# A streaming encoder layer: the channel mean of a LayerNorm summed by accumulating matmuls instead of vector adds

## What is computed

```
h = rmsnorm(x);  q, k, v, u_a, u_b, gates = split(h @ w_in)
u = u_a * sigmoid(u_b)
y = causal_depthwise_conv(u, width 31) + b_dw        # 1024 channels
mu = mean(y, over the 1024 channels)                 # one mean per token
yc = y - mu
y  = yc * rsqrt(mean(yc*yc) + 1e-6) * ln_g + ln_b
conv = silu(y) @ w_conv_out
m = sigmoid(gA) * attention(q, k, v) + sigmoid(gB) * conv
x = x + rmsnorm(m @ w_out);  x = x + rmsnorm(swiglu(rmsnorm(x)))
```

## Time and profile before

| | |
|---|---|
| time, median of 3 runs (range) | 3239.17 us (3236.28 to 3239.52) |
| the profiled execution: time, span | 3239.52 us, 3237.4 us |
| mean granted TensorE clock | 0.991 |
| TensorE matmul busy | 3144.0 us, 97% |
| VectorE busy | 1555.5 us, 48% |
| ScalarE, GpSimd busy | 1065.4 us (33%), 511.7 us (16%) |
| the chain that ended last | TensorE 79%, VectorE 3%, ScalarE 2% |

### The profile page before, as it was taken

How to read it: one execution, slowest core, us unless ns; L and a number is a source line. 1 busy time by engine, 2 the same in 40 slices (tenths; PEclk the granted TensorE clock), 3 DMA queues, 4 the chain that set the end, 5 groups by cost and what they waited for, 6 DMA issues and landing times.

```text
span 3237.4 us, 42868 instructions
## 1 busy us (share of the span) xinstructions
PE 3144.0 (97%) x16983; PEld 2683.5 (83%) x16983; DVE 1555.5 (48%) x2757; ACT 1065.4 (33%) x1905; POOL 511.7 (16%) x543
## 2 busy tenths in 40 slices
PE   8989989999999999999999999999999999999998
PEld 6768878878887878888887888888899898899987
DVE  7987754445796631003497652002289655200013
ACT  5666432234346421003255532002235542200012
POOL 4930000000471000000083000000057100100000
PEclk9999999999999999999999999999999999999999
DMA  8864568777653355555554344555554332445443
GB/s 279 279 222 170 220 238 293 284 279 283 227 188 137 118 194 183 190 188 208 216 187 169 118 169 175 189 195 208 184 197 176 135 114 109 166 172 182 170 156 125
DMA packets 176486, 622.66 MB, mean 192 GB/s; under 512 B 20656, under 2 KB 26672, under 8 KB 175776
## 3 DMA queue, kind: packets, MB, share of 16 engines
q1 hardware_dynamic: 175328, 619.53, 53.3%
q10 hardware_dynamic: 960, 0.40, 0.0%
HBM read 480.41 MB, written 139.54 MB: 191 GB/s over the span
## 4 chain that ended last, share of the span: by engine, by line
PE 79%; DVE 3%; ACT 2%; DMA 1%; POOL 1%; issue 1%; SPq 0%; DVEq 0%; POOLq 0%; ACTq 0%
PE PS L791 51%; PE PS L843 7%; PE PS L845 7%; PE PS L844 7%; PE PS L825 2%; PE PS L932 2%; PE PS L920 1%; DVE PS L1466 1%; PE PS L951 1%; POOL sq_sum L733 1%; PE PS L952 1%; PE PS L953 1%; PE PS L772 1%; DMA out_y_prompt<-x 1%; ACT act_hi L1238 0%
## 5 line engine op out<-in xcount | busy, mean ns | idle before, releaser
L791 PE MATMUL PS<-h_hi,w_hi 128*128 128x512 f32 (+1 forms) x3328 | 1064.3, 353 | 17.0 <-DVE u L1711 3.9
L791 PE MATMUL PS<-h_hi,w_lo 128*128 128x512 f32 (+1 forms) x3328 | 1065.1, 353 | 0.0
L791 PE MATMUL PS<-h_lo,w_hi 128*128 128x512 f32 (+1 forms) x3328 | 1054.8, 350 | 0.0
L791 PEld LDWEIGHTS PS<-h_hi,w_hi 128*128 128x128 f32 x3328 | 586.0, 189 | 101.9 <-issue 21.2
L791 PEld LDWEIGHTS PS<-h_lo,w_hi 128*128 128x128 f32 x3328 | 585.1, 189 | 90.7 <-issue 1.7
L791 PEld LDWEIGHTS PS<-h_hi,w_lo 128*128 128x128 f32 x3328 | 586.4, 189 | 82.0
L727 POOL TENSOR_TENSOR y<-y,prod 128x512 f32<-128x512 f32 (+1 forms) x333 | 408.4, 1253 | 188.8 <-ACT prod L1216 176.5
L1466 DVE SCALAR_TENSOR_TENSOR PS<-u,dw,PS 128x512 f32<-128x512 f32 (+1 forms) x604 | 434.6, 775 | 7.0
L1868 DVE TENSOR_TENSOR f<-PS,tmp 128x512 f32<-128x512 f32 (+1 forms) x88 | 61.5, 698 | 662.0 <-PE PS L791 643.3
L843 PE MATMUL PS<-w_hi,f_hi 128*128 128x512 f32 x748 | 297.7, 398 | 5.8 <-DVE f L1868 5.4
L845 PE MATMUL PS<-w_hi,f_lo 128*128 128x512 f32 x748 | 295.3, 395 | 0.0
(11 more groups left out here) (195 smaller groups left out, 3631.2 us busy)
## 6 DMA issues: line engine op xcount, KB each, us to landing
w_lo<-lo_dram SPq DMA_DIRECT2D x372, 512.0 KB, 4.3
w_hi<-hi_dram SPq DMA_DIRECT2D x372, 512.0 KB, 3.3
w_raw<-in_w_stream SPq DMA_DIRECT2D x124, 512.0 KB, 4.6
hi_dram<-w_hi SPq DMA_DIRECT2D x124, 512.0 KB, 4.4
lo_dram<-w_lo SPq DMA_DIRECT2D x124, 512.0 KB, 3.9
x<-in_x_prompt SPq DMA_DIRECT2D x4, 2048.0 KB, 12.4
xs<-in_x_prompt SPq DMA_DIRECT2D x12, 512.0 KB, 5.1
out_y_prompt<-x SPq DMA_DIRECT2D x3, 2048.0 KB, 10.6
```

Of the source, the lines that this page charges most:

```text
L791: last = nc.tensor.matmul(PS[:, k0 + off, 0:n], w, x[:, k, c0:c0 + n], start=first and k == 0, stop=stop and k == KT - 1)
```

## The change

The sum over the channel tiles is no longer made by VectorE. TensorE multiplies `ones` with each of the 8 tiles of y itself and lets the products accumulate in the same PSUM bank. In blocks 0 to 2 five of the eight matmuls (tiles 0, 2, 4, 1, 3) are issued at ln 1, two steps earlier than before, and three (tiles 6, 7, 5) at ln 3. In block 3 all eight are issued at ln 3. Before each tile TensorE waits for the tap that ends it, in place of the one wait for `y_summed`. The wait for the residual of the block before (`pn_ok`) moves with the first of them.

```
-            def channel_means(b, ypieces):
-
-                pe.wait_ge(y_summed, b + 1)
-                for c0, n, off in ypieces:
-                    last = nc.tensor.matmul(PS[:, mean_bank(b) + off, 0:n], ones[:], sq_sum[:, c0:c0 + n],
-                                            start=True, stop=True)
-                last.then_inc(mu_done, 1)
+            def channel_means(b, ypieces, cts, first, last_one):
+
+                for ct in cts:
+                    if vector_taps(b, ct) < TAPS:
+                        pe.wait_ge(prod_used, adds_done(b, ct))
+                    else:
+                        pe.wait_ge(conv_step, taps_done(b, ct))
+                    for c0, n, off in ypieces:
+                        last = nc.tensor.matmul(PS[:, mean_bank(b) + off, 0:n], ones[:], y[:, ct, c0:c0 + n],
+                                                start=first and ct == cts[0], stop=last_one and ct == cts[-1])
+                if last_one:
+                    last.then_inc(mu_done, 1)
...
-                        if ln == 3:
+                        if ln == 1 and not ext(b):
                             if b:
                                 pe.wait_ge(pn_ok, post_tile(b - 1, tiles(b - 1) - 1, 1) + 1)
-                            channel_means(b, ypieces)
+                            channel_means(b, ypieces, (0, 2, 4, 1, 3), True, False)
+                        if ln == 3 and not ext(b):
+                            channel_means(b, ypieces, (6, 7, 5), False, True)
+                        if ln == 3 and ext(b):
+                            channel_means(b, ypieces, (0, 2, 4, 1, 3, 6, 7, 5), True, True)
...
-            def sum_tiles(b):
-
-                yw = YW if ext(b) else T
-                dve.wait_ge(conv_step, taps_before(b + 1))
-                total, rest = sq_sum[:, 0:yw], (4, 6, 7, 1, 3, 5)
-                link(TT(total, y[:, 0, 0:yw], y[:, 2, 0:yw], ALU.add))
-                for ct in rest:
-                    if vector_taps(b, ct) < TAPS:
-                        dve.wait_ge(prod_used, adds_done(b, ct))
-                    ins = TT(total, total, y[:, ct, 0:yw], ALU.add)
-                    if ct != rest[-1]:
-                        link(ins)
-                ins.then_inc(y_summed, 1)
...
-                    if ln == 3:
-                        sum_tiles(b)
```

More of the change, by code:

```diff
@@ L218, in build @@
         sbias_in = sem("sbias_in")
-        y_summed = sem("y_summed")
         yn_ok, ahi_ok, afull_ok, alo_ok = sem("yn_ok"), sem("ahi_ok"), sem("afull_ok"), sem("alo_ok")
```

## The result

| | before | after |
|---|---|---|
| median of the timed runs, us | 3238.86 (3236.28 to 3239.52, 4 runs) | 3257.41 (3253.90 to 3260.78, 4 runs) |
| profiled execution: time, span | 3239.52, 3237.4 | 3250.26, 3248.2 |

The ratio is 1.0059, 95% interval 1.0046 to 1.0072: 19 us slower, with 15 to 23 in the interval. Forecast were 3254 us and a range of 3246 to 3262. The profiled execution of the changed kernel is the fastest of all its executions, only 10.7 us above its counterpart; the first experiment shows much of what made it so.

The account below looks back on a forecast made before the run. The prediction took TensorE, busy 97% of the span, to bound the kernel. Its terms, -2.1 us in block 0, +11.0 in blocks 1 and 2, +5.8 in block 3, gave +14.7: 3254 us, range 3246 to 3262.

Parts of the forecast that it names:

- What bounds the kernel: Whole kernel: TensorE's matmuls cover 97% of the span, so work added there costs its full price.
- The price of a mean, 0.88 us and 1.09: TensorE's issue time per mean: 0.88 us in block 1, 1.09 us in block 3 with its two matmuls.
- Blocks 1 and 2, +5.5 each: Per block, seven more means cost 6.16 us and a shorter wait for the squares returns 0.65 us.
- Block 3, +5.8: In block 3, seven more means cost 7.6 us and a shorter wait for the squares returns 1.8 us.
- Block 0, -2.1: In block 0, losing the stall for VectorE's sum and the reduced clock behind it gains 2.1 us.
- The stretch of 14.68 us: Block 0 before: end of step 28 to end of next step, 14.68 us, against 12.57 us after.
- it moves with that step and stays: Block 0's wait before the squares follows ScalarE's last three squares, so it was to remain unchanged.
- The moved waits at ln 1: TensorE's waits for tiles 0, 2, 4, 1, 3 cost nothing, with a margin of 4.9 us in block 1.
- The cheap mean: Rival: successive means overlap down to 0.46 us each, giving 3242.4 us, no visible difference; chance 0.08.
- the late tile: Rival: GpSimd finishes tile 3 late, TensorE stands some 4 us per block at ln 1, 3270 us or above; chance 0.06.
- The faster rival: Rival: VectorE's freed time shortens the start of attention, -11.2 us, to 3228 us; chance 0.05.
- the rivals that give "the same": Outcomes within 0.2%: cheap means, chance 0.08, and a partial gain at attention's start, 0.04; stated together as 0.10.

Follow-up runs that it names:

- the first experiment: The changed kernel run again with no edit, against the kernel before: 3257.39 us, ratio 1.0054.
- the added half alone: The kernel before with its one mean matmul issued eight times at ln 3, VectorE's sum kept: 3262.5 us, ratio 1.0071.
- the removed half alone: The kernel before without VectorE's sum, its one mean matmul taking tile 7 alone: 3235.5 us, ratio 0.9991.

## Why the prediction was right, point by point

- *What bounds the kernel.* Right. With the added half alone +23 us, with the removed half alone -3 us, and by its trace none of that in blocks 1 to 3 up to the squares, where the sum was hidden under TensorE.
- *The price of a mean, 0.88 us and 1.09.* Right: 0.858 and 1.08 in sequence. The Trainium skill's isolated gap of 0.216 us for a matmul of 512 columns ("TensorE: Matmul & The Clock Gate", "Back-to-back issue gap") would be 0.43 for the two records of a mean, and the run with doubled means shows twice that. For the ordinary matmuls, 0.230 us apart, the same rule is nearly right.
- *Blocks 1 and 2, +5.5 each.* Right: +5.4 in the trace, 10.4 us timed for the two. The waits for squares fell to 0.63 us (0.75 forecast).
- *Block 3, +5.8.* Right up to the squares, +5.8. A little came back behind them that was not in the sum. After a stall of 2.6 us the two profiles of the kernel before ran at the lower clock, after one of 0.67 us the changed kernel did not. First the second profile of the kernel before, then the changed one, windows that begin behind the squares:

```profile
2526.00:2528.00 2.00, 2.00 (x7) 1.30 (x8) 0.41 (x1) 0.00 (x0) 0.00 (x0) 0.66 0.71 281
2528.00:2530.00 2.00, 2.00 (x10) 2.00 (x10) 1.18 (x3) 1.57 (x3) 0.00 (x0) 0.50 0.00 0
```

```profile
2546.00:2548.00 2.00, 2.00 (x11) 1.52 (x12) 0.75 (x2) 1.27 (x1) 0.00 (x0) 1.00 0.81 277
2548.00:2550.00 2.00, 2.00 (x18) 2.00 (x17) 1.18 (x2) 1.91 (x3) 0.00 (x0) 1.00 0.62 248
```

  Ten and eighteen matmuls in the same two microseconds; about 1.5 us in all. It is not certain to happen: of six profiles with a single mean in block 3, three had the lower clock behind that stall (of 2.60, 2.61 and 2.55 us) and three kept the higher (2.52, 2.54 and 2.62 us). The length of the stall does not tell which.
- *Block 0, -2.1.* This is the term that was mis-sized. The trace of the changed kernel shows -1.2 against the first profile of before and -0.2 against the second (190.62 to 210.31, 19.69 us); the timed part is +1.9 with an interval from -1 to +5. Three things were wrong in it. First, a row was misread. 209.28 is not the start of the step's last matmul:

```profile
208.82 0.39 PE L791 MATMUL PS<-h_hi,w_lo 128*128 128x512 f32 x1
209.05 0.39 PE L791 MATMUL PS<-h_hi,w_hi 128*128 128x512 f32 x1
209.28 0.39 PE L791 MATMUL PS<-h_lo,w_hi 128*128 128x512 f32 x1
```

  The step's 24 matmuls start at 201.59 to 208.82, and 209.28 is the second one of the next step. The stretch of 14.68 us is 14.22, and the term -1.65. Second, the step "it moves with that step and stays", on the wait for the squares, failed: the wait grew by 0.62 us, and by 3.0 us in the run without a sum, since GpSimd's chain of additions is what it hangs on once the mean comes early. With the eight means 0.02 us cheaper each (0.18), that closes the account against the first profile: -1.65 + 0.62 - 0.18 = -1.21. Third, the stall and the reduced clock behind it were read from one execution, and its stall was the longest of the five profiles that have it.
- *The moved waits at ln 1.* Right: no wait in front of the five, and the time does not depend on their place.
- *The rivals.* The cheap mean and the late tile did not happen. The faster rival, VectorE's time as attention's gain, fell with the run without a sum: its waits at attention's start are 9.4 us in blocks 1 to 3, as before, and 3.0 and 3.3 us in block 0. Three small sums do not fit each other, and none changes the verdict: means at 1.04 us would add 28 x 0.16 = 4.5 us and not 3.9; a mean at which the change falls to 6.5 us is 0.59 us and not 0.57; and the rivals that give "the same" have chances of 0.08 and 0.04, 0.12 in sum and not 0.10.

The sum came to 14.7 us. The trace gives -1.2 + 5.4 + 5.4 + 5.8 = 15.4 to the squares and some 14 with the clock behind them; timed are 17.5 to 19, some 3 to 4 us above both the forecast and the trace. The error in block 0 makes 1 us, and block 3's clock gave 1.5 back, so that the forecast total agrees with the trace in part by luck. Those 3 to 4 us stay open. Some 0.7 us may be the longer wait for weights in block 2, which no run isolates. The rest is no mean and no matter of placement, by the runs above; three profiles of one program end 11 us apart, in stretches of lower clock, in block 3's pace and in block 0's convolution, and the profiles are too few to say which of these leans to one side.

## What to carry to other kernels

Ask first which engine is full: an addition that an idle engine makes under it costs nothing (here in blocks 1 to 3), and eight fp32 matmuls for one do. A stall that is removed often hangs on a second chain that starts at the same point; before its whole length is counted as gain, look for the next wait and for what feeds it. And read a stall's length from more than one execution before it enters a sum.

## What the runs showed of the hardware that was not expected

- The same program, at a granted clock of 1.00 throughout, ran block 3's feed-forward part at 11.95, 12.05 or 12.11 us per pair of steps, one value for the whole part in each execution. It makes up to 3 us.
- An fp32 matmul of 512 columns costs 0.858 us in a run, nearly what it costs alone (0.88), and 3.7 times an fp32r one (0.230 us).
- The same stall before block 3's squares, 2.5 to 2.6 us long, was followed by the lower clock in three of six profiles and not in the other three.
